# Two transformer blocks on one core: attention ends reordered, norm chains by halves, two up products for three

## The reference, cut

```
# x: 256 tokens x 1024, float32 throughout
for i in range(2):                                   # first_block
    m = neighborhood_attention(rms_norm(x, g0)) if i == 0 else diff_attention(rms_norm(x, g0))
    x = x + rms_norm(m @ w_o, g1)
    gate, val = split(rms_norm(x, g2) @ w_in)        # 2 x 2816 columns
    x = x + rms_norm((gelu(conv3(gate)) * val) @ w_out, g3)
    x = x + sigmoid(rms_norm(x, g4) @ w_gate) * (p[i] @ w_proj)
x = x + 0.5 * (silu(n(x) @ w1_gate) * (n(x) @ w1_up)) @ w1_down      # second_block
x = x + concat(hgrn2(n(x) @ w_in), mla(n(x) @ w_in)) @ w_out
x = x + 0.5 * (silu(n(x) @ w2_gate) * (n(x) @ w2_up)) @ w2_down
x = x + sigmoid(n(x) @ w_ple_gate) * (p_2 @ w_ple_proj)
return rms_norm_2(x, ln_final)
```

## Time and profile before

| | us |
|---|---|
| median of 3 runs | 1406.74 (1406.55 to 1407.74) |
| the profiled execution | 1408.87 |
| its span in the profile | 1407.3 |
| TensorE matmul busy | 1264.3 (90%) |
| VectorE busy | 826.4 (59%) |
| ScalarE busy | 629.0 (45%) |

### The profile page before, as it was taken

One profiled execution on the slowest core, in us unless ns is written; L12 is line 12 of the kernel. 1 busy time (PEld: TensorE's weight loads), 2 busy tenths in 40 slices (PEclk: granted clock), 3 DMA queues, 4 the chain that ended last, 5 costly groups with the idle time before them and its releaser, 6 DMA issues. The chain is left out here.

```text
span 1407.3 us, 19395 instructions
## 1 busy us (share of the span) xinstructions
PE 1264.3 (90%) x8145; PEld 1144.0 (81%) x8145; DVE 826.4 (59%) x921; ACT 629.0 (45%) x854; POOL 108.2 (8%) x216
## 2 busy tenths in 40 slices
PE   6997769999999776699999979999889987999997
PEld 5887669999878764599998779999767776999995
DVE  6645346666776654566666845555456775444455
ACT  5634334444465552344444644434354643333444
POOL 4000030000010000100000100000015321000000
PEclk9999889999999989899999989999999998999999
DMA  9631155555447320265554525555243324655550
GB/s 287 210 115 63 58 158 180 180 180 180 180 165 233 115 73 30 86 203 192 191 188 151 187 90 182 188 193 193 84 149 113 131 72 149 202 180 180 180 176 35
DMA packets 148730, 214.62 MB, mean 153 GB/s; under 512 B 4378, under 2 KB 114396, under 8 KB 148644
## 3 DMA queue, kind: packets, MB, share of 16 engines
q1 hardware_dynamic: 145356, 205.62, 43.9%
q0 software_dynamic: 1632, 4.71, 1.3%
q10 hardware_dynamic: 1656, 3.05, 0.6%
HBM read 212.30 MB, written 1.06 MB: 152 GB/s over the span
## 5 line engine op out<-in xcount | busy, mean ns | idle before, releaser
L953 DVE TENSOR_TENSOR w_lo<-raw,w_hi 128x2048 fp32r<-128x2048 f32 (+1 forms) x195 | 445.1, 2289 | 213.2 <-PE work L1421 131.2
L1419 PE MATMUL work<-hT_hi,w_hi 128*128 128x256 f32 x1696 | 488.7, 288 | 11.1 <-DVE hT_lo L964 6.1
L1420 PE MATMUL work<-hT_lo,w_hi 128*128 128x256 f32 x1696 | 485.6, 286 | 0.0
L1421 PE MATMUL work<-hT_hi,w_lo 128*128 128x256 f32 x1696 | 485.3, 286 | 0.0
L615 ACT ACTIVATE w_hi<-raw 128x2048 fp32r<-128x2048 f32 (+1 forms) x195 | 368.3, 1894 | 10.8 <-DMA raw<-in_na_w_qkv 9.4
L1419 PEld LDWEIGHTS work<-hT_hi,w_hi 128*128 128x128 f32 x1696 | 331.6, 195 | 19.8 <-issue 16.7
L1420 PEld LDWEIGHTS work<-hT_lo,w_hi 128*128 128x128 f32 x1696 | 331.5, 195 | 3.1
L1421 PEld LDWEIGHTS work<-hT_hi,w_lo 128*128 128x128 f32 x1696 | 331.1, 195 | 0.0
L1419 PE MATMUL acc<-w_hi,aux_hi 128*128 128x512 f32 x384 | 151.6, 395 | 6.5 <-DVE aux_lo L1209 3.6
L1420 PE MATMUL acc<-w_lo,aux_hi 128*128 128x512 f32 x384 | 150.5, 392 | 0.0
L1421 PE MATMUL acc<-w_hi,aux_lo 128*128 128x512 f32 x384 | 149.5, 389 | 0.0
(11 more groups left out here) (201 smaller groups left out, 1421.5 us busy)
## 6 DMA issues: line engine op xcount, KB each, us to landing
raw<-in_ffn_w_in SPq DMA_DIRECT2D x44, 1024.0 KB, 5.7
raw<-in_ffn_w_out SPq DMA_DIRECT2D x22, 1024.0 KB, 5.0
raw<-in_w_gate SPq DMA_DIRECT2D x22, 1024.0 KB, 5.4
raw<-in_w_up SPq DMA_DIRECT2D x22, 1024.0 KB, 5.8
raw<-in_w_down SPq DMA_DIRECT2D x22, 1024.0 KB, 4.9
raw<-in_na_w_qkv SPq DMA_DIRECT2D x12, 1024.0 KB, 6.7
raw<-in_da_w_qkv SPq DMA_DIRECT2D x12, 1024.0 KB, 5.3
raw<-in_ple_w_gate SPq DMA_DIRECT2D x8, 1024.0 KB, 5.1
```

Source lines behind the costliest of these rows:

```text
L953: dve.tensor_tensor(w_lo[:, n % RING, 0:size], raw[:, n % RAW, 0:size], w_hi[:, n % RING, 0:size].bitcast(F32), ALU.subtract).then_inc(lo_ ...
L1419: pe.matmul(dst, stationary[0], moving[0], start=first, stop=False)
L1420: pe.matmul(dst, stationary[0], moving[1], start=False, stop=False)
L1421: return pe.matmul(dst, stationary[1], moving[0], start=False, stop=last)
```

## The change

Five edits, made together.

1. Late units. Unit 6's scores move from half-column 15 to 14 and use accumulators 0 and 1. The tails become lists of their own for each block; projection pieces stand in other places, all four K pieces follow each other, and turn_x of the first tile comes after the last of them.
2. Norm chains by halves. Squares, the first GpSimd step, gain product, residual update and final store work on 512 columns each. post multiplies acc by the gain before rstd is there, then scales and adds in one operation.
3. The calls of feed in the ends of phases move: on VectorE mostly after normed or tile_parts, on ScalarE after pre.
4. Merged up products. hT_hi and hT_lo lie side by side in hT_both. One matmul of 512 columns multiplies w_hi with both, one of 256 columns w_lo with hT_hi; gate and up take a bank each, and VectorE adds the two halves of each bank with tensor_reduce.
5. down_done counts four quarters of the last block instead of two tiles.

The diff, cut to its core:

```diff
-SCORED = [3, 4, 7, 8, 11, 12, 15]
+SCORED = [3, 4, 7, 8, 11, 12, 14]
...
-    first = [] if ph == 0 else [("V", 5)]
-    return first + [("P", (0, 0)), ("S", 7), ("P", (0, 1)), ("T", 6), ("P", (1, 0)), ("V", 6), ("T", 7),
-                    ("P", (1, 1)), ("V", 7), ("O", 1), ("K", (0, 0)), ("K", (0, 1)), ("K", (1, 0)), ("K", (1, 1))]
+    late = {0: [("S", 7), ("P", (0, 0)), ("T", 6), ("P", (0, 1)), ("V", 6), ("T", 7), ("P", (1, 0)), ("V", 7), ("O", 1),
+                ("P", (1, 1))],
+            3: [("S", 7), ("P", (0, 0)), ("V", 5), ("P", (0, 1)), ("T", 6), ("P", (1, 0)), ("V", 6), ("T", 7), ("V", 7),
+                ("P", (1, 1)), ("O", 1)]}[ph]
+    return late + [("K", (0, 0)), ("K", (0, 1)), ("K", (1, 0)), ("K", (1, 1))]
...
         def score_bank(u):
-            return 2 * (u % 2) if u < 6 else 2
+            return 2 * (u % 2)
...
                 for t in range(T):
-            sp.dma_start(out[0, t * P:(t + 1) * P, :], xn[:, t, :]).then_inc(stored, 16)
+                for q in range(2):
+                    sp.dma_start(out[0, t * P:(t + 1) * P, half], xn[:, t, half]).then_inc(stored, 16)
...
+                    if halves:
+                        pool.wait_ge(sq_done, squares - 1)
+                        link(pool.tensor_scalar(ms[:, c + 1:c + 2], ssq[:, c:c + 1], scale, EPS, ALU.mult, ALU.add))
+                        pool.wait_ge(sq_done, squares)
+                        link(pool.tensor_scalar(ms[:, c:c + 1], ssq[:, c + 1:c + 2], scale, ms[:, c + 1:c + 2],
+                                                ALU.mult, ALU.add))
...
             def end_of_acc(ph, b, finish):                      # ScalarE
                 feed(b + 5)
                 finish(0)
-                feed(b + 6)
+                feed(b + 7 if PHASES[ph] in ("na", "da") else b + 6)
                 pre(ph + 1, 0)
                 tile_parts(ph + 1, 0)
                 finish(1)
-                feed(b + 7)
                 pre(ph + 1, 1)
+                feed(b + 7)
...
             def post(ph, t):                                    # VectorE
+                for q in range(2):
+                    dve.wait_ge(sq_done, EV[i][2] - 1 + q)
+                    ins = dve.tensor_tensor(xn[:, t, half], acc[:, 2 * t + q, :], gb[:, half], ALU.mult)
+                link(ins)
+                dve.wait_ge(rstd_done, i + 1)
+                for q in range(2):
+                    dve.scalar_tensor_tensor(out=x[:, t, half], in0=xn[:, t, half], scalar=rstd[:, c:c + 1],
+                                             in1=x[:, t, half], op0=ALU.mult, op1=ALU.add).then_inc(x_ready, 1)
...
             def end_of_acc(ph, b, finish):                      # VectorE
                 feed(b + 5)
                 finish(0)
+                normed(ph + 1, 0)
                 feed(b + 6)
-                normed(ph + 1, 0)
                 tile_parts(ph + 1, 0)
                 finish(1)
-                feed(b + 7)
                 normed(ph + 1, 1)
                 if ph + 1 == 3:
                     feed(b + 8)
                 tile_parts(ph + 1, 1)
+                feed(b + 7)
...
                     full(dve, g)
+                    dve.tensor_reduce(src, bank(g).rearrange("p (e s) -> p s e", e=2), AX.X, ALU.add)
...
+                    full(dve, g + 1)
+                    dve.tensor_reduce(hid, bank(g + 1).rearrange("p (e s) -> p s e", e=2), AX.X, ALU.add)
...
-                if kh == 1 and t == 1 and half == 0:
+                if kh == 1 and t == 1 and half == 1:
                     turn_x(ph + 1, 0)
...
                     for i in range(2):
+                        v, b = slab(n + i), open_bank(pe, g + i)
                         for k in range(KT):
-                            ins = product3(b[:, cols(i, S)], both(v, every, k, cols(c % 2)), both(hT, every, k, every),
-                                           k == 0, k == KT - 1)
+                            pe.matmul(b.rearrange("p (e s) -> p e s", e=2), v[0][:, k, cols(c % 2)], hT_both[:, k, :, :],
+                                      start=k == 0, stop=False)
+                            ins = pe.matmul(b[:, 0:S], v[1][:, k, cols(c % 2)], hT_hi[:, k, :],
+                                            start=False, stop=k == KT - 1)
```

More of the change, by code:

```diff
@@ L742, in attention @@
                     weights_turned(ph, u)
-                if ph == 3:
-                    for u in after(ph, gap(ph, HALVES - 1), "V") + [5]:
-                        head_squares(ph, u)
-                unit_exps(ph, 6)
-                feed(wo + 5)
-                unit_exps(ph, 7)
-                weights_turned(ph, 6)
-                if ph == 3:
+                if ph == 0:
+                    weights_turned(ph, 6)
+                    unit_exps(ph, 7)
+                    weights_turned(ph, 7)
+                else:
+                    for u in after(ph, gap(ph, HALVES - 1), "V"):
+                        head_squares(ph, u)
+                    unit_exps(ph, 7)
+                    head_squares(ph, 5)
+                    weights_turned(ph, 6)
+                    weights_turned(ph, 7)
                     head_squares(ph, 6)
-                weights_turned(ph, 7)
-                if ph == 3:
                     head_squares(ph, 7)
+                feed(wo + 6)
                 output_parts(ph, 1)
@@ L781, in ffn @@
                     else:
-                        full(act, g)
-                        act.activation(glu[:, c % 2, :], bank(g)[:, 0:S], ACT.Silu).then_inc(act_done, 1)
+                        evacuated(act, g)
+                        act.activation(glu[:, c % 2, :], gsum[:, c % 2, :], ACT.Silu).then_inc(act_done, 1)
                     if c % 2 == 0:
@@ L1135, in attention @@
                             scaled_outputs(ph, 0)
-                scores(ph, 6)
                 if ph == 0:
@@ L1140, in attention @@
                     expand(7)
-                feed(wo + 5)
-                if ph == 3:
-                    weights(ph, 6)
                 scores(ph, 7)
@@ L1148, in attention @@
                 else:
+                    weights(ph, 6)
                     weights(ph, 7)
@@ L1410, in _ @@
                 dve.wait_ge(gb_loaded, 16 * 6)
-                dve.scalar_tensor_tensor(out=xn[:, t, :], in0=x[:, t, :], scalar=rstd[:, c:c + 1], in1=gb[:, :],
-                                         op0=ALU.mult, op1=ALU.mult).then_inc(out_ready, 1)
+                for q in range(2):
+                    half = slice(q * 512, (q + 1) * 512)
+                    dve.scalar_tensor_tensor(out=xn[:, t, half], in0=x[:, t, half], scalar=rstd[:, c:c + 1],
+                                             in1=gb[:, half], op0=ALU.mult, op1=ALU.mult).then_inc(out_ready, 1)
         @block.tensor
@@ L1587, in output_piece @@
                     pe.wait_ge(part_ready, H[f"o{ph}.{kh}"] - 1 + t)
-                if kh == 0 and t == 1 and half == 0:
-                    pe.wait_ge(s_free, units_before[ph] + UNITS)
+                if kh == 0 and half == 0:
+                    pe.wait_ge(s_free, units_before[ph] + UNITS - 1 + t)
                 v = slab(B[f"wo{ph}"] + 2 * kh + half)
```

138 lines of the change are left out of this document (73 added, 65 removed).

## The result

The changed kernel takes 1368.7 us (median; 1367.2 to 1371.1) beside 1407.2 us for the kernel before on the same chip, a ratio of 0.9728 (95% interval 0.9711 to 0.9745). The gain is 38.5 us where 50.6 had been forecast; the time lies 12.5 us above the predicted 1356.2, inside the range that ends at 1373 and 0.7 us above the band of 1341 to 1368 that had been given a chance of 0.72. The profiled execution has a span of 1369.3 us against 1407.3.

What follows compares the result with a forecast made beforehand. TensorE, busy 1264 of 1407 us, was taken as the bound, with gains in product cost and chains between phases. Terms summed to 50.6 us, from 1408.9 to 1358.3 profiled, 1356.2 as median; range 1341 to 1373.

Steps and rivals of the forecast that it cites:

- Merged up products: Feed-forward up stages: two products for three, 0.348 us for 0.360 a step, 1408 steps, 16.4 us gained.
- Rival (b): Up stages: merging saves next to nothing, the 12 ns belonging to weight changes or columns; 1370 us, chance 0.04.
- Reductions: VectorE in feed-forwards: two 0.69 us reductions per block, hidden with about 1 us to spare per pair of 16.6 us.
- (a): Conv-GLU pairs: short reductions cost 1.22 us each, 24 us lost, SwiGLU still hidden; 1380 us, chance 0.12.
- (d): Feed-forwards: reductions with 256 outputs take 2.07 us, VectorE bounds both kinds, 132 us lost; 1488 us, chance 0.03.
- the walk: Following engine queues piece by piece to time feed-forward pairs and attention block ends; the two tail walks may each miss by 3 us.
- wait for aux_lo: Conv-GLU ends: the last down product's 0.9 us wait shrinks with the early gate; 1.0 us counted for two ends.
- Norm chains and the stretch to the up stage: Attention blocks' ends, projection to up stage: half-size norm steps and four consecutive pieces gain 9.0 (neighborhood) and 7.4 us (differential).
- Late units: Attention block tails: unit 6's earlier scores and moved projection pieces gain 6.8 us (differential) and 2.8 us (neighborhood).
- the wait of V5: Neighborhood tail: scores(6) ahead of output(4), which releases V5, makes V5 wait about 3 us.
- Entry of the differential block: Gated layer to differential block: two weight slabs converted after the norm, the third piece waits for one; 0.3 us lost.
- Rival (c): Reordered ends gain less because a passed queue sets a new wait; half of 26 us lost, 1369 us, chance 0.08.

Runs made afterwards that it cites:

- the three-product kernel: Changed kernel with the up stage back at three products of 256 columns a step in all four feed-forwards; 1380.9 us, ratio 0.9794.
- The doubled reductions: Changed kernel with every halved reduction issued twice on VectorE, the second into a spare tile, 176 more reductions; 1386.8 us, ratio 0.9831.
- the first changed one: First profiled execution of the unedited changed kernel, against the kernel before: median 1368.7 us, ratio 0.9728, span 1369.3 us; measured again later at 1366.6 us.

## Why the prediction was right, and what it missed

**Merged up products.** The mechanism was right, the size off: 16.4 us forecast, 9.9 measured (88 stages). The failed term is 0.228 + 0.120 = 0.348. The two durations are right, each behind its like; in turn they make 0.353, and of the 12 ns that a merge should save 7 are left. Rival (b), no gain from merging, falls by the three-product kernel. The Trainium skill (TensorE: Matmul & The Clock Gate, Back-to-back issue gap) gives N/2.4 + 2.5 ns for the isolated gap. In the streams of this case it is 227 to 229 ns for 512 columns and 119 to 120 for 256, 12 to 15 ns above N/2.4, so the traces do not bear out its constant here.

**Reductions.** 0.69 us forecast, 0.687 measured, hidden as the pairs' count said; a pair holds 13.5 us of VectorE work (81% of 16.8) where 14.4 had been summed. Rivals (a) and (d) fall with that number. The doubled reductions add a warning to the walk: at about 1.37 us per reduction 16 us show, not the 24 and more of (a)'s reckoning, and they show in the end of each conv-GLU, as a wait and the low clock behind it, far more than in its pairs. The 0.9 us wait for aux_lo in a conv-GLU's end, of which I took 0.5 off each, shrank by 0.25 in one and not in the other.

**Norm chains and the stretch to the up stage.** 9.0 and 7.4 forecast; 9.8 and 9.2 from the projection half on, but only 8.0 and 6.7 in the stretch that was forecast, since the second tile's turn_x starts 15.1 us after the first tile's pieces in place of the walk's 14.1 (neighborhood). The other 4.3 us are the clock of the pieces, for which the forecast had 1.0. That the two rows come out at their size or above is in part luck. The experiments give the stretch parts: gain products beside the root 2.5 us each, no conversion in the second tile's chain 1.4 each, the turn behind the last piece 0.6 and 2.2. Half squares were not taken apart, so what is left of the gain has no cause shown.

**Late units.** Differential: 6.8 forecast, 7.5 measured; putting the old order back costs 9.1 with the clock behind it. Neighborhood: 2.8 forecast, 0.2 measured in the tail; the wait of V5 was named and sized (about 3, measured 2.87), but the step failed in taking its cost for the wait alone. The 3.4 us of low clock behind it were counted nowhere: the forecast gave the clock a gain of 1.0 for pauses that go and no loss for the ones that it brought in. Both numbers are too small, 4.3 gained in the projections and up to 6.3 lost behind the two new waits.

**Entry of the differential block.** The third piece's wait was named as well, at a net 0.3; it is 2.7 us, with 0.7 at the first piece beside it. The conversion that it needs starts on VectorE only behind the second tile's norm, at 406.14, when the two pieces that should cover it have ended (405.83), so its 2.29 us are all exposed. Behind it the clock fell in six of ten executions, 1.6 us more in five of them and 2.9 in the first changed one. The kernel before had 1.6 us of low clock at this entry too, so at equal clock the order alone costs 4.0.

**Rival (c),** the ends doing half of the walk at 1369, has the measured time. As a whole it does not hold: the ends gave 27 us where 26 had been walked, 4.3 of them clock. Its mechanism is there in one place, scores(6) ahead of output(4), which costs 6.0 us with its clock, not 13. The shortfall is 6.5 us of the merge and 5 at an entry that had been priced at 0.3. By the prediction's own numbers the low end of the range would be 1342.6, not 1341 (1356.2 less 4.6, 3.0 and 6).

## What to carry to other kernels

Take the price of a product from a stream with the same order of widths, and issue products of one width behind one another where the accumulation allows it. Price each wait that an order brings in with the clock that may fall behind it: here waits of 2.6 to 3 us cost up to 3.4 us more. Keep long two-input conversions on VectorE out of a chain that goes through a small GpSimd step, and move whatever a norm doesn't need the root for into the time in which the root is made.

## What the runs showed of the hardware

- A GpSimd step on one column that starts while VectorE converts w_lo (two SBUF inputs, 2048 elements) ends 0.05 us after the conversion. It is so for every L510 step that starts inside one in the changed kernel: 0.64 us at 158.58, 1.71 at 365.33, 1.39 at 535.61 and 1.70 at 743.39, against 0.19 alone. The Trainium skill (GPSIMD Engine Reference, Specifications) says that GpSimd's SBUF interfaces are shared with VectorE, with contention where a VectorE instruction has two SBUF inputs; the trace agrees, and its number is 2.06 us for a 0.19 us step.
- A 512-column product costs 7 ns more in turn with 256-column ones than among its like (235.8 against 228.6 ns), a 256-column one 2 ns less.
- The clock behind the same wait of 2.6 us was 0.53 in one execution and 1.00 in another of the same kernel, while behind V5's 2.7 to 3.0 it was low in each of the nine executions in which the wait stood. Behind the 1.63 us wait ahead of the differential projection half, the next 24 products took 7.2 us in five of the eleven traces with the new tail and 5.6 in the six others. What decides it stays open, and a difference of 1.6 to 3 us at such a place says nothing of an edit.
